# Second mixer: the scores of two near or two sparse heads of one tile become one step

## The reference, cut to what matters

```
h = rmsnorm(x, mix_norm) @ w_in
o_a = chunk_relpos_attention(...)    # "near": 6 heads of 64, bias by distance
o_b = dsa_attention(...)             # "sparse": 5 heads of 64, keys picked by an index score (top 64)
o_c = mla_attention(...)             # "latent": 5 heads of 64 + 32, low-rank q and kv
x = x + concatenate([o_a, o_b, o_c]) @ w_out
```

## Time and profile before

| | us |
|---|---|
| median of 3 runs | 1905.72 |
| lowest, highest run | 1900.38, 1912.37 |
| span of the profiled execution | 1904.3 |
| PE busy in it | 1878.8 |
| DVE busy | 1198.5 |
| ACT busy | 1007.6 |

### The profile page before, as it was taken

One profiled execution on the slowest core, in us unless ns is written; L12 is line 12 of the kernel. 1 busy time (PEld: TensorE's weight loads), 2 busy tenths in 40 slices (PEclk: granted clock), 3 DMA queues, 4 the chain that ended last, 5 costly groups with the idle time before them and its releaser, 6 DMA issues.

```text
span 1904.3 us, 31110 instructions
## 1 busy us (share of the span) xinstructions
PE 1878.8 (99%) x12720; PEld 1599.7 (84%) x12720; DVE 1198.5 (63%) x2473; ACT 1007.6 (53%) x2054; POOL 91.6 (5%) x187
## 2 busy tenths in 40 slices
PE   9999999999999999999999999999999999999998
PEld 7888888888888788888888887888888888878887
DVE  5576555666654656766675765667565757656565
ACT  5565554423312555645565666556555656665554
POOL 0000000212210000010000000000000000000000
PEclk9999999999989999999999999999999999999999
DMA  6555443122202355635463342556355733435552
GB/s 237 188 210 210 178 155 111 68 96 71 71 30 96 114 205 178 251 106 195 177 250 113 130 151 94 178 195 251 125 177 179 261 104 129 149 111 188 185 189 112
DMA packets 42717, 296.12 MB, mean 156 GB/s; under 512 B 4832, under 2 KB 4960, under 8 KB 10576
## 3 DMA queue, kind: packets, MB, share of 16 engines
q1 hardware_dynamic: 41184, 288.32, 42.6%
q0 software_dynamic: 1392, 5.83, 0.9%
HBM read 293.08 MB, written 1.05 MB: 154 GB/s over the span
## 4 chain that ended last, share of the span: by engine, by line
PE 94%; DVE 3%; ACT 1%; POOL 1%; issue 1%; DMA 0%; SPq 0%; POOLq 0%; DVEq 0%; ACTq 0%
PE PS L1605 21%; PE PS L1547 16%; PE PS L1549 15%; PE PS L1548 15%; PE PS L1607 11%; PE PS L1556 1%; PE PS L2049 1%; PE PS L1825 1%; PE PS L1844 1%; PE PS L1837 1%; PE PS L1582 1%; PE PS L1741 1%; PE PS L1961 1%; DVE wlo L2453 1%; PE PS L2038 1%
## 5 line engine op out<-in xcount | busy, mean ns | idle before, releaser
L2453 DVE TENSOR_TENSOR wlo<-raw,whi 128x512 fp32r<-128x512 f32 (+5 forms) x784 | 614.2, 826 | 199.1 <-ACT whi L2092 193.0
L1605 PE MATMUL PS<-xhl,whi 128*128 128x512 f32 x1728 | 613.4, 399 | 0.0
L2092 ACT ACTIVATE whi<-raw 128x512 fp32r<-128x512 f32 (+5 forms) x784 | 533.4, 735 | 142.5 <-PE PS L1549 139.2
L1607 PE MATMUL PS<-xhl,wlo 128*128 128x256 f32 x1728 | 485.0, 281 | 0.0
L1605 PEld LDWEIGHTS PS<-xhl,whi 128*128 128x128 f32 x1728 | 324.7, 188 | 79.4
L1607 PEld LDWEIGHTS PS<-xhl,wlo 128*128 128x128 f32 x1728 | 326.3, 189 | 2.1
L1547 PE MATMUL PS<-whi,yh 128*128 128x512 f32 (+2 forms) x572 | 225.7, 395 | 0.0
L1548 PE MATMUL PS<-wlo,yh 128*128 128x512 f32 (+2 forms) x572 | 221.9, 388 | 0.0
L1549 PE MATMUL PS<-whi,yl 128*128 128x512 f32 (+2 forms) x572 | 221.8, 388 | 0.0
L2538 DVE TENSOR_TENSOR arena<-arena,PS 128x256 f32<-128x256 f32 x216 | 90.2, 418 | 159.5 <-ACT arena L2162 159.5
L1547 PE MATMUL PS<-whi,xhl 128*128 128x512 f32 (+4 forms) x480 | 189.6, 395 | 0.5 <-DVE wlo L2453 0.3
(11 more groups left out here) (273 smaller groups left out, 2519.0 us busy)
## 6 DMA issues: line engine op xcount, KB each, us to landing
raw<-wall SPq DMA_DIRECT2D x249, 1024.0 KB, 4.9
raw<-wall SPq DMA_DIRECT2D x12, 768.0 KB, 4.2
raw<-wall SPq DMA_DIRECT2D x8, 968.0 KB, 4.9
raw<-wall SPq DMA_DIRECT2D x4, 896.0 KB, 4.6
arena<-ebias POOLq DMA_DIRECT2D x2, 768.0 KB, 4.6
raw<-wall SPq DMA_DIRECT2D x2, 720.0 KB, 4.4
raw<-wall SPq DMA_DIRECT2D x2, 640.0 KB, 4.2
X<-x SPq DMA_DIRECT2D x2, 512.0 KB, 6.1
```

The lines of the kernel that those rows point to most:

```text
L1605: e.matmul(b, hi[:, c0:c0 + 128], xhl[:, k, :, :].rearrange("p a t -> p (a t)"), start=(k == 0), stop=False, skip_group_check=True)
L1607: p = e.matmul(b[:, 0:256], lo[:, c0:c0 + 128], xh[:, k, :], start=False, stop=(k == 7), skip_group_check=True)
L2092: e.activation(whi[slot_of(i)][:, c].bitcast(F32R), raw[i % 3][:, c], copy).then_inc(*M.sig("whi", ("split", i, q)))
L2453: e.tensor_tensor(wlo[slot_of(i)][:, c], raw[i % 3][:, c], whi[slot_of(i)][:, c].bitcast(F32), ALU.subtract).then_inc(*M.sig("wlo", *[("ha ...
```

## The change

A new chain `score` takes the scores and the exps of two heads of one tile (near: 0-1, 2-3, 4-5; sparse: 0-1, 2-3, 4 alone) as one step: it waits until there are slots and banks for both, issues both scores, then both exps. For latent heads it takes one head. `unit` no longer makes the score: it waits until its head is scored, and goes on with the turning of the weights and the sum as before. The PE price of a near or sparse score in `PACE` goes from 0.6 to 0.35.

Since heads may now end in another order, the first one that comes to its sum takes the bank, the last one starts `u_norm`, and `u_norm` waits for all heads. `outs` now waits for the products 2 and 3 as well, before it turns any output.

```diff
-    "u_score_b": (("pe", 0.6), ("dve", 0.4)), "u_score_a": (("pe", 0.6), ("dve", 0.4)), "u_soft": (("act", 0.45),),
+    "u_score_b": (("pe", 0.35), ("dve", 0.4)), "u_score_a": (("pe", 0.35), ("dve", 0.4)), "u_soft": (("act", 0.45),),
...
+        def score(kind, hs, tt):
+
+            us = [(kind, h, tt) for h in hs]
+            S = self.slots["N" if kind == "a" else "S", s]
+            while kind not in made or kind == "b" and "mask" not in made or min(len(S.free), len(st.free)) < len(us):
+                yield 1
+            yield from self.room(len(us))
+            for u in us:
+                S.take(u)
+                st.take(u)
+                self.turn(("us", s) + u, "u_score_" + kind, s, *u[1:])
+            for u in us:
+                self.do("u_soft", s, *u)
+                scored[u] = self.ready
+            yield 1
...
         def unit(kind, h, tt, n):
             u = (kind, h, tt)
             S = self.slots["N" if kind == "a" else "S", s]
-            while kind not in made or kind == "b" and "mask" not in made or not (S.free and st.free):
-                yield 1
-            S.take(u)
-            st.take(u)
-            yield from self.room(1)
-            self.turn(("us", s) + u, "u_score_" + kind, s, h, tt)
-            self.do("u_soft", s, kind, h, tt)
-            yield 1
+            while u not in scored:
+                yield 1
+            self.ready = max(self.ready, scored[u])
...
-            if h == 0:
+            if (kind, tt) not in summed:
                 yield from self.room(1)
+            if (kind, tt) not in summed:
                 self.bank.take(("pv", s, kind, tt))
-            self.do("u_out", s, kind, h, tt)
+                summed[kind, tt] = 0
+            summed[kind, tt] += 1
+            self.do("u_out", s, *u)
...
-            if h == n - 1:
+            if summed[kind, tt] == n:
...
-                while not {(kind[0], tt) for tt in tts} <= heads:
+                while not ({(kind[0], tt) for tt in tts} <= heads and {2, 3} <= made):
...
-        units = [unit(kind, h, tt, n) for kind, n in (("a", 6), ("c", 5), ("b", 5)) for tt in range(2) for h in range(n)]
+        units = []
+        for kind, n, m in (("a", 6, 2), ("c", 5, 1), ("b", 5, 2)):
+            for tt in range(2):
+                for h in range(0, n, m):
+                    units.append(score(kind, range(h, min(h + m, n)), tt))
+                    units += [unit(kind, i, tt, n) for i in range(h, min(h + m, n))]
...
-                for t in due(h == 0 and bank_free(tile), ("act", ("pt", s) + u), got[kind], ("pool", ("zz", s))):
+                for t in due(bank_free(tile), ("act", ("pt", s) + u), got[kind], ("pool", ("zz", s))):
...
-                for t in due(("pe", ("pv", s, kind, n - 1, tt))):
+                for t in due(*[("pe", ("pv", s, kind, h, tt)) for h in range(n)]):
```

More of the change, by code:

```diff
@@ L1014, in mix2 @@
     def mix2(self, s, l):
-        made, heads = set(), set()
+        made, heads, scored, summed = set(), set(), {}, {}
         def proj(j):
@@ L1045, in unit @@
             yield from self.room(1)
-            self.turn(("ut", s) + u, "u_turn", s, kind, h, tt)
+            self.turn(("ut", s) + u, "u_turn", s, *u)
             yield 1
```

## The result

| | us |
|---|---|
| predicted | 1911.0 (1899 to 1919) |
| after, median of 20 runs | 1906.61 (1904.41 to 1919.77) |
| before, median of 20 runs beside it | 1900.39 (1898.99 to 1912.91) |
| after to before | 1.0031, 95% interval 1.0016 to 1.0046 |
| profiled execution after: time, span, mean granted clock | 1913.5, 1911.4, 0.993 |

The change costs about 6 us, a third of a per cent: within the 1% that was called no change, and of the sign and size that was forecast (+5.4).

The account below looks back on a forecast made before the run. PE, busy 1878.8 of 1904.3 us, bounds the kernel. Per mixer -2.2 - 0.6 - 0.9 + 2.3 + 3.2 + 0.6 + 0.3 = +2.7 us, two mixers +5.4, so 1905.7 becomes 1911 (range 1899 to 1919).

Parts of the forecast that it names:

- What pairing is worth: Near and sparse scores on PE: the second head of a pair costs nothing, saving 2.2 and 0.6 us per mixer.
- near term of 2.2: Near heads: runs of tile 0 from four to three, of tile 1 from five to three, -2.2 us per mixer.
- the change of mode: Alternative price of a run: only the array's drain of 0.19 us goes with each, 0.8 us per mixer.
- Waits that go: PE's old waits at two latent transposes of tile 1 and the three-head sparse run vanish, -0.9 us per mixer.
- Waits that come: New PE waits after P3, at a latent sum, turn_b and the sparse part: 2.3, 3.2, 0.6 and 0.3 us per mixer.
- the sum 2.3: First wait: head 3's latent sum waits 2.3 us for ACT's copy, queued behind exp, DVE's score and two split pieces.
- turn_b 3.2: Second wait: turn_b on PE waits 3.2 us for DVE's second brope, starting at T + 10.2.
- sparse transpose 0.6: Transpose of the first sparse head, right behind four scores, waits 0.6 us for its exp.
- the 0.3 at the sparse outputs: First turned sparse outputs wait about 0.3 us for their norm, behind two scores at 256 keys on DVE.
- rival 2: The clock falls in PE's new gaps, adding 1.75 to 3.5 us per mixer: 1914 to 1918; chance 0.25.
- Rival 1: New mixer waits stay small, turn_b's under 1 us, kernel a little faster: 1902, or 1898 with none; chance 0.29.
- Rival 3: Clock stays low through the sparse heads to the stage's end, up to 10 us per mixer: 1925 or more; chance 0.03.

Follow-up runs that it names:

- e9: Kernel of e2 with pairs for the near scores alone, sparse scores taken one by one: median 1900.15 us, mixers 141.71 and 142.34.
- e2: Changed kernel, but the sums let no split pieces of wout2 chunk 3 in between the end of P3 and turn_b: median 1901.86 us.
- e3: Changed kernel with other partners (0 and 2, 1 and 3), so both scores of these pairs lie on the same half of the partitions: median 1913.06 us.
- e5: Changed kernel with the turning of the latent heads held back until the products P2 are done: median 1911.81 us.
- e8: Kernel before, no pairs, with the price 0.35 per near or sparse score and turned outputs gated at P3's fourth column block: median 1911.95 us.
- e1: Changed kernel with blank products in PE's two new gaps per mixer, 9 ahead of a latent sum and 14 ahead of turn_b: median 1908.14 us.
- e10: Kernel of e2 with all scores single, same functions and same price of 0.35: median 1908.38 us.
- e11: Kernel of e2 with the gate of e4 added, so outputs are turned from P3's fourth column block: median 1903.49 us.
- e4: Changed kernel with the gate of the turned outputs opened at P3's fourth column block instead of its end: median 1904.07 us.
- e12: Kernel of e2 with before's price of 0.6 per near or sparse score in place of 0.35: median 1901.81 us.

## Why the prediction came out right, point by point

**What pairing is worth: the price of a run is right, the sum a little too large.** The near scores stand as six runs of four records, 0.49 and 0.70 long, as forecast. Timeline of PE after, one pair of each tile between dense products:

```profile
1088.94 0.34 PE L1568 MATMUL PS<-whi,xhl 128*128 128x384 f32 x1
1089.21 0.49 PE L2032 MATMUL PS<-arena 64*128 64x128 f32 x4
1089.63 0.44 PE L1566 MATMUL PS<-whi,xhl 128*128 128x384 f32 x1
1089.91 0.34 PE L1567 MATMUL PS<-wlo,xhl 128*128 128x384 f32 x1
...
1103.38 0.31 PE L1568 MATMUL PS<-whi,yl 128*128 128x320 f32 x1
1103.62 0.70 PE L2032 MATMUL PS<-arena 64*128 64x256 f32 x4
1104.26 0.41 PE L1566 MATMUL PS<-whi,yh 128*128 128x320 f32 x1
1104.50 0.31 PE L1567 MATMUL PS<-wlo,yh 128*128 128x320 f32 x1
```

From product to second product behind the pair it is 0.97 and 1.12 us, where two steps of these products would pass in 0.35 and 0.29: a pair costs 0.62 and 0.83 us, what the prediction had for a single head. With nine runs before and six now that is its near term of 2.2. For the whole, take the listed waits out of a mixer, and what the fall cost (1.4 in the first, by which turn_b's wait is shorter there, and 1.6 in the second): before 141.1 and 141.4 are left, after 138.6 and 139.2. The work shrank by 2.6 and 2.2 us, forecast was 2.2 + 0.6 = 2.8. The split into near and sparse is not isolated by any run: e9, with the near pairs alone, has 2.1 and 1.8 less than before, e2, with the change's pairs but its sparse scores in six runs, only 1.3 and 1.1. If the change of mode were all that goes with a run, as the prediction weighed, 0.8 would have gone, by its estimate from the rows. The Trainium skill (TensorEngine Tiling (Array Packing), Key Properties) names the drain at such a change, not its size. The 0.8 doesn't fit, for the second head's own time goes as well, as e3 shows from the other side.

**Waits that go: right.** None of the earlier trace rows is left.

**Waits that come: right in place, cause and order but for the smallest, a fifth too large.** Forecast and measured per mixer: the sum 2.3 and 1.77; turn_b 3.2 and 2.62 (1.22 where the slow clock fell into it); sparse transpose 0.6 and 0.69; the 0.3 at the sparse outputs did not come, and 0.16 stood at a sparse transpose (L2057) instead. In sum 6.4 and 5.2. The first came out smaller because PE's own work ran to about T + 2.4 and ACT's copy was in at T + 4.1, not 4.5; the second, because DVE's chain ended at T + 9.6 and not 10.2, while PE was through at T + 7.0 as forecast. A wait that the list didn't have grew from 0.2 to 0.5 at dense products that need a split piece (L1566). e2 shows the cause as the prediction named it.

**The clock: rival 2's mechanism took place together with the forecast's.** They were set against each other as if one excluded the other; in the profiled execution the clock fell in both mixers. So the forecast's own condition, no fall, did not hold there; only the price of the fall was small. It said 1.75 to 3.5 us per mixer, and that a stretch in the second wait is hidden; the second half of that is what the first mixer shows, and where the fall comes behind turn_b it is 1.6, a little under the lower end. The Trainium skill (TensorE: Matmul & The Clock Gate, HAM oscillation) has waits of PE bring the throttle back; the trace agrees for the change, e5 and e8, while e9 waited as long as 0.9 us at turn_b without a fall. In e1, e10 and e11 the same waits stand in both mixers and the clock fell in one of them only.

**The sum, near by luck in part.** The second mixer grew by 4.00: old waits -0.9, new waits +5.2, the waits for split pieces +0.3, the fall +1.6, which leaves -2.2 for the work. The first grew by 2.04: the fall lies ahead of turn_b's wait and is free, turn_b's wait is shorter by the 1.4 that PE's work is longer, and -2.6 is left for the work. Together +6.0; forecast +5.4. The new waits, counted as they are where no fall cuts them short, were 2.3 us too high in the forecast; the one fall that cost something (1.6), the waits for split pieces (0.6) and the smaller saving of work (0.8), none of which it had, make that up and more.

**The number.** 1911.0 against 1906.61. Of the 4.4 us, 5.3 come from the base: the three runs of before gave a median of 1905.72, twenty gave 1900.39. The change's own +6.2 is 0.8 above the forecast's +5.4. So what the number is off by is its base, the middle one of three runs that happened to lie in three different groups (last section). The 1.4 us that was laid between span and median is the distance of two executions (in the execution after, time and span are 2.1 us apart), but it stands on both sides of the sum, which doesn't hang on it.

Rival 1 (1898 to 1902) fell: turn_b waited 2.62 us, not under 1. Rival 3 fell: each slow stretch ended after 3.4 us, before the sparse heads began.

## What to carry to other kernels

A step that is made shorter on the busiest engine gives nothing if a later step of that engine waits for another engine's queue; so follow, for each wait in the new order, everything that stands ahead of its releaser on that releaser's engine, and price that chain, not the engine's own saving. The cheapest repair is often not more filler but fewer bystanders: holding back four split pieces brought back more than 4 of 6 us (1.6 of them the fall of the clock that no longer came), while blanks and held-back heads brought nothing. And compare a stage's own length in the trace where the whole kernel's time scatters by more than the change.

## What the runs showed that was not expected

- Runs of one kernel come in groups: before near 1900, 1906 and 1912.5, after near 1905.5, 1911.5 and 1919.5. The profiled executions differ in a slow stretch of the clock that starts at 547 to 550 us, far ahead of the two mixers and outside the change: 3.4 us long in e1 (1907.95), 13.7 in before (span 1904.3), 17.1 in after (1913.5) and e2 (1909.07), 30.7 in e4 (1916.62) and e12 (1913.71), and absent in e9 (1899.53). That this stretch alone makes the groups is not shown, for only one execution of each kernel is profiled. A median over few runs picks a group. The earlier trace rows show where before's stretch begins.
- A fall of the clock inside a chain that ends in a wait is free; the same fall behind the wait cost 1.6 us (the two mixers of after) and 1.5 (e1).
- A second head of 64 rows costs 0 us on the other half of the partitions and 0.22 or 0.43 us on the same half, at 128 and 256 keys (e3).
